# Four edits at the head of a decoder-block kernel: the bias table skewed by a replicated line in DRAM, the gate columns as one packed tile, one tile's squares on VectorE, the first key chunk between the gate products

## The reference, cut to what matters

```python
D_MODEL = 1024; SEQ = 512; N_HEADS_A = N_HEADS_B = 8; CHUNK_B = 64; CONV_B = 4
...
h = rmsnorm(x, attn_norm[i])
proj = h @ w_in[i]
qa, ka, va, qb, kb, vb, zb, bb, ab, gl = jnp.split(proj, cuts, axis=-1)
...
oa = diff_attention(qa, ka, va, lam, rel_bias)        # logits + bias_table[rel_bucket(q_pos - k_pos)]
qkv = jax.nn.silu(causal_dwconv(jnp.concatenate([qb, kb, vb], axis=-1), conv_b[i]))
qb, kb, vb = jnp.split(qkv, ...)
beta = jax.nn.sigmoid(bb)
g = -jnp.exp(a_log_b[i]) * jax.nn.softplus(ab + dt_bias_b[i])
ob = gated_delta_rule(qb, kb, vb, g, beta)            # g summed along each chunk of 64 tokens
gates = jax.nn.sigmoid(gl)
mixed = gates[:, :, 0] * (oa @ w_br_a[i]) + gates[:, :, 1] * (ob @ w_br_b[i])
x = x + mixed @ w_out[i]
x = x + (jax.nn.silu(ug) * uv) @ w_down[i]            # ug, uv from a second norm, w_up and a conv
x = x + jax.nn.sigmoid(h @ w_ple_gate[i]) * (p[i] @ w_ple_proj[i])
```

## Time and profile before

| | |
|---|---|
| median of 3 runs | 1159.39 us |
| all runs | 1157.6, 1159.39, 1159.72 us |
| the profiled execution | 1160.82 us, of which its span is 1159.0 us |
| busy | TensorE 1123.9 us, VectorE 655.2, GpSimd 633.1, ScalarE 549.4 |
| the chain that ended last | TensorE 87%, VectorE 9%, ScalarE 3% |
| line 562, the three-pass matmuls | 75% of that chain |

### The profile page before, as it was taken

One profiled execution on the slowest core, in us unless ns is written; L12 is line 12 of the kernel. 1 busy time (PEld: TensorE's weight loads), 2 busy tenths in 40 slices (PEclk: granted clock), 3 DMA queues, 4 the chain that ended last, 5 costly groups with the idle time before them and its releaser, 6 DMA issues.

```text
span 1159.0 us, 16765 instructions
## 1 busy us (share of the span) xinstructions
PE 1123.9 (97%) x5502; PEld 898.7 (78%) x5502; DVE 655.2 (57%) x1036; ACT 549.4 (47%) x886; POOL 633.1 (55%) x769
## 2 busy tenths in 40 slices
PE   6998989999999999999999999999999999999997
PEld 4786667777777777667878888888888888888886
DVE  4668976767666776862213324476776515731534
ACT  5584647566565656551322124544444314433542
POOL 6386264546554564645456554566576754573452
PEclk9999999999999999999999999999999999999999
DMA  8354031331404123213223523333333432332232
GB/s 243 77 132 130 26 94 35 85 85 35 102 18 118 38 64 100 75 54 85 79 77 105 181 72 91 91 93 114 103 90 91 116 102 73 109 96 80 74 89 79
DMA packets 196619, 104.36 MB, mean 90 GB/s; under 512 B 3926, under 2 KB 195401, under 8 KB 196553
## 3 DMA queue, kind: packets, MB, share of 16 engines
q1 hardware_dynamic: 196172, 103.39, 32.0%
q10 hardware_dynamic: 381, 0.15, 0.1%
HBM read 101.40 MB, written 2.13 MB: 89 GB/s over the span
## 4 chain that ended last, share of the span: by engine, by line
PE 87%; DVE 9%; ACT 3%; issue 1%; ACTq 0%; DVEq 0%
PE bank L562 75%; PE bank L698 2%; PE bank L712 1%; DVE prod L1810 1%; DVE xs L1812 1%; PE bank L705 1%; PE bank L657 1%; DVE pr L1722 1%; PE bank L922 1%; DVE pr L1721 0%; DVE oa_lo L1978 0%; PE bank L909 0%; PE bank L919 0%; PE bank L910 0%; PE bank L913 0%
## 5 line engine op out<-in xcount | busy, mean ns | idle before, releaser
L492 POOL TENSOR_TENSOR w_lo<-w_raw,w_hi 128x256 fp32r<-128x256 f32 x692 | 549.9, 828 | 259.9 <-ACT w_hi L1074 254.2
L562 PE MATMUL bank<-hn_hi,w_hi 128*128 128x512 f32 x1000 | 408.4, 408 | 1.0 <-DVE o_a L1985 1.0
L562 PE MATMUL bank<-hn_hi,w_lo 128*128 128x512 f32 x1000 | 391.0, 391 | 0.0
L562 PE MATMUL bank<-hn_lo,w_hi 128*128 128x512 f32 x1000 | 390.4, 390 | 0.0
L562 PEld LDWEIGHTS bank<-hn_hi,w_hi 128*128 128x128 f32 x1000 | 189.0, 189 | 43.7 <-issue 9.2
L562 PEld LDWEIGHTS bank<-hn_hi,w_lo 128*128 128x128 f32 x1000 | 187.9, 188 | 40.4
L562 PEld LDWEIGHTS bank<-hn_lo,w_hi 128*128 128x128 f32 x1000 | 188.7, 189 | 34.6 <-issue 1.7
L507 POOL CAST w_hi<-w_raw 128x1024 fp32r<-128x1024 f32 x70 | 78.2, 1117 | 222.0 <-PE bank L562 131.3
L1074 ACT ACTIVATE w_hi<-w_raw 128x1024 fp32r<-128x1024 f32 x111 | 117.9, 1062 | 77.6 <-PE bank L562 69.7
L2096 DVE SCALAR_TENSOR_TENSOR u<-vr,pt,u 128x511 f32<-128x511 f32 x88 | 88.9, 1010 | 8.3 <-DVE u L2096 0.7
L2090 DVE TENSOR_TENSOR vr<-bank,rs 128x512 f32<-128x512 f32 x44 | 30.4, 692 | 72.5 <-PE bank L562 67.1
(11 more groups left out here) (308 smaller groups left out, 1643.6 us busy)
## 6 DMA issues: line engine op xcount, KB each, us to landing
w_raw<-in_w_in SPq DMA_DIRECT2D x73, 512.0 KB, 6.7
w_raw<-in_w_up SPq DMA_DIRECT2D x44, 512.0 KB, 3.8
w_raw<-in_w_down SPq DMA_DIRECT2D x16, 512.0 KB, 3.9
crow<-cum_rows_out SPq DMA_DIRECT2D x16, 256.0 KB, 5.7
w_raw<-in_w_br_a SPq DMA_DIRECT2D x8, 512.0 KB, 4.0
w_raw<-in_w_br_b SPq DMA_DIRECT2D x8, 512.0 KB, 4.0
w_raw<-in_w_out SPq DMA_DIRECT2D x8, 512.0 KB, 3.9
w_raw<-in_w_ple_gate SPq DMA_DIRECT2D x8, 512.0 KB, 4.0
```

Of the source, the lines that this page charges most:

```text
L492: ins = pool.tensor_tensor(wlo[c.slot][:, ks, :], raw[c.slot][:, ks, :], whi[c.slot][:, ks, :].bitcast(F32), ALU.subtract)
L562: mm = pe.matmul(acc, w[c.slot][:, i, :], xx[:, x0 + i, :], start=(i == 0 and n == 0), stop=last)
```

## The change

- **Order of loads.** The constants are loaded after the second tile of `x` in place of the first, and are 48 KB shorter (no flipped identity, but a small pick matrix of 16 columns). The gate columns are loaded as 16 columns only, in rows of 64 bytes; the first key chunk comes right behind them, ahead of the lines of the bias.
- **Squares.** VectorE takes the squares of the second tile of `x`; ScalarE takes the other three, and the inverse roots of the second and third tile come together, after the third tile's squares.
- **Gate columns packed.** GpSimd puts the high part of the 16 columns in columns 0 to 15 of a buffer and the low part in 16 to 31. One matmul with 32 stationary columns serves high and low: two matmuls for each row block where there were three. A matmul with the pick matrix both turns the result and adds the two halves, in place of the transpose on line 624.
- **First key between.** The first three row blocks of the gates come first, then a step of the first key chunk (in bank 1) and a row block of the gates in turn. Of the filler then stand: 2 steps; gates turned, and here the bias line (line 611, moved; its copy on VectorE moves behind the gates' additions); 5 steps; the running sums; 2 steps; the sums turned; 1 step; then the heads as before.
- **Bias.** The bias line is written to DRAM 128 times for each head (1.5 MB in one DMA, its source 8 partitions). A read whose step from partition to partition is one number less than a line puts the bias straight into `bias`. `slope`, the flipping matmuls and the copies are gone. VectorE waits for the landing after `scale_rows`.
- **Order on SyncE.** Four key chunks go ahead of the line's write, the sixth behind it; the bias is read after the loads of all keys; each row load of the running sums moves one chunk load later.

```diff
             for t in range(NT):
                 sp.dma_start(x_tok[:, t, :], ...)
-                if t == 0:
-                    sp.dma_start(sq[:, :], consts[:, 0:C_HOT * P]).then_inc(sem("consts_in"), 16)
-            load(stream.ba.at(0), w_in0, COLS["ba"])
+                if t == 1:
+                    sp.dma_start(sq[:, :], consts[:, 0:C_HOT]).then_inc(sem("consts_in"), 16)
+            sp.dma_start(raw[0][:, :, 0:16], gate_cols).then_inc(arrived[0], 16)
+            load(stream.keys.at(0), w_in0, COLS["kb"])
...
-            for n in (1, 2):
+            for n in (1, 2, 3, 4):
                 load(stream.keys.at(n), w_in0, COLS["kb"] + n * P)
             sp.wait_ge(sem("line_ready"), 1)
-            sp.dma_start(dram_line, line[:, :]).then_inc(sem("line_out"), 16)
-            sp.wait_ge(sem("line_out"), 16)
-            skew = bass.AP(tensor=dram_line.tensor, offset=0, ap=[[1, P], [LINE, H], [1, 256]])
-            sp.dma_start(slope[:, :, :], skew).then_inc(sem("slope_in"), 16)
-            for n in (3, 4):
-                load(stream.keys.at(n), w_in0, COLS["kb"] + n * P)
+            sp.dma_start(dram_line, line[:, :].unsqueeze(1).to_broadcast([H, P, LINE])).then_inc(sem("line_out"), 16)
+            load(stream.keys.at(5), w_in0, COLS["kb"] + 5 * P)
...
+            sp.wait_ge(sem("line_out"), 16)
+            skew = bass.AP(tensor=dram_line.tensor, offset=P - 1, ap=[[LINE - 1, P], [P * LINE, H], [1, 256]])
+            sp.dma_start(bias[:, :, :], skew).then_inc(sem("bias_in"), 16)
...
+            def gate_products(i):
+                pe.wait_ge(low_ready, 1)
+                pe.wait_ge(sem("h_split"), i + 1)
+                for n, xx in enumerate((hn_hi, hn_lo)):
+                    mm = pe.matmul(bank[0][0:32, :], whi[0][:, i, 0:32], xx[:, i, :], ...)
-            run(gemm(stream.ba.at(0), hn_hi, hn_lo, ready=("h_split", 0)))
+            f = Fill(gemm(stream.keys.at(0), hn_hi, hn_lo, ready=("h_split", 0)))
+            for i in range(3):
+                gate_products(i)
+            for i in range(KD):
+                f.step(1)
+                if i + 3 < KD:
+                    gate_products(i + 3)
...
             for t in range(NT):
-                mm = pe.transpose(bank[5][:, t * 16:t * 16 + 16], ba_sb[:, t * P:(t + 1) * P], ident[0:16, 0:16])
+                mm = pe.matmul(bank[5][:, t * 16:t * 16 + 16], ba_sb[:, t * P:(t + 1) * P], pick[0:32, :], ...)
             mm.then_inc(sem("ba_T"), 1)
-            f.step(6)
+            pe.matmul(bank[6][0:H, 0:LINE], tab[:, :], hot[:, :], start=True, stop=True).then_inc(sem("line_mm"), 1)
+            f.step(5)
             pe.wait_ge(sem("ba_gates"), 4)
...
-            f.step(2)
-            pe.wait_ge(sem("slope_in"), 16)
-            for n in range(H // 2):
-                pe.matmul(bank[6 + n % 2][:, :], flip, slope[:, 2 * n:2 * n + 2, :]..., ...)
-            f.step(4)
+            f.step(1)
...
-            for t in range(NT):
+            for n, (t, t0) in enumerate(((0, 0), (2, 1), (3, 3))):
                 act.wait_ge(sem(f"x_in{t}"), 16)
                 link(nc.scalar.activation(junk[:, :], x_tok[:, t, :], ACT.Square, accum_out=ss0[:, t:t + 1]))
...
+            dve.wait_ge(sem("x_in1"), 16)
+            done(V.scalar_tensor_tensor(out=junk1[:, :], in0=x_tok[:, 1, :], scalar=1.0, in1=x_tok[:, 1, :],
+                                        op0=ALU.mult, op1=ALU.mult, accum_out=ss0[:, 1:2]), "x_sq", 1)
...
-                if h == 0:
-                    for n in range(H // 2):
-                        bias_copy(n)
```

More of the change, by code:

```diff
@@ L190, in const @@
             return sq[:, n * P:(n + 1) * P]
-        ident, flip, cum, half, ones, mask = map(const, range(6))
+        ident, cum, half, ones, mask = map(const, range(5))
+        pick = sq[:, C_PICK:C_HOT]
         LOW, UP = slice(0, HEAD), slice(HEAD, P)
@@ L229, in build @@
         lamp = sb("lamp", [P, 2, 64], F32, first)
-        ba_sb = sb("ba_sb", [16, T], F32, first)
+        ba_sb = sb("ba_sb", [32, T], F32, first)
         cum_rows = sb("cum_rows", [NT * H, P], F32, first)
-        junk = sb("junk", [P, D], F32, first)
+        junk, junk1 = (sb(n, [P, D], F32, first) for n in ("junk", "junk1"))
         alog = sb("alog", [P, H], F32, first)
@@ L608, in _ @@
                         mm.then_inc(sem("x_T"), 1)
-            pe.wait_ge(sem("lines_in"), 16 * 2)
-            pe.wait_ge(sem("eps_set"), 4)
-            pe.matmul(bank[6][0:H, 0:LINE], tab[:, :], hot[:, :], start=True, stop=True).then_inc(sem("line_mm"), 1)
             for c in range(len(IN_BANKS), KD):
@@ L616, in _ @@
                 mm.then_inc(sem("x_T"), 1)
-            run(gemm(stream.ba.at(0), hn_hi, hn_lo, ready=("h_split", 0)))
-            f = Fill(*[gemm(stream.keys.at(n), hn_hi, hn_lo) for n in range(H)],
+            def gate_products(i):
+                pe.wait_ge(low_ready, 1)
+                pe.wait_ge(sem("h_split"), i + 1)
+                for n, xx in enumerate((hn_hi, hn_lo)):
+                    mm = pe.matmul(bank[0][0:32, :], whi[0][:, i, 0:32], xx[:, i, :],
+                                   start=(i == 0 and n == 0), stop=(i == KD - 1 and n == 1))
+                if i == KD - 1:
+                    mm.then_inc(product_ready, 1)
+            f = Fill(gemm(stream.keys.at(0), hn_hi, hn_lo, ready=("h_split", 0)))
[5 more added lines that the diff above has]
+                    gate_products(i + 3)
+            f = Fill(*[gemm(stream.keys.at(n), hn_hi, hn_lo) for n in range(1, H)],
                      *[gemm(stream.first.at(n), hn_hi, hn_lo) for n in range(len(FIRST))])
@@ L623, in _ @@
             for t in range(NT):
-                mm = pe.transpose(bank[5][:, t * 16:t * 16 + 16], ba_sb[:, t * P:(t + 1) * P], ident[0:16, 0:16])
+                mm = pe.matmul(bank[5][:, t * 16:t * 16 + 16], ba_sb[:, t * P:(t + 1) * P], pick[0:32, :], start=True, stop=True)
             mm.then_inc(sem("ba_T"), 1)
-            f.step(6)
+            pe.wait_ge(sem("lines_in"), 16 * 2)
+            pe.wait_ge(sem("eps_set"), 4)
+            pe.matmul(bank[6][0:H, 0:LINE], tab[:, :], hot[:, :], start=True, stop=True).then_inc(sem("line_mm"), 1)
+            f.step(5)
             pe.wait_ge(sem("ba_gates"), 4)
@@ L1094, in _ @@
             act.wait_ge(sem("eps_set"), 3)
[L1095 removed]
+            for n, (t, t0) in enumerate(((0, 0), (2, 1), (3, 3))):
                 act.wait_ge(sem(f"x_in{t}"), 16)
                 link(nc.scalar.activation(junk[:, :], x_tok[:, t, :], ACT.Square, accum_out=ss0[:, t:t + 1]))
[L1098 to L1099 removed]
+                if t == 2:
+                    act.wait_ge(sem("x_sq"), 1)
+                these = slice(t0, t + 1)
+                link(nc.scalar.activation(lnx[:, these], ss0[:, these], ACT.Ln, bias=sm[:, 28:29], scale=1.0 / D))
+                done(nc.scalar.activation(rs0[:, these], lnx[:, these], ACT.Exp, scale=-0.5), "x_r", n + 1)
             act.wait_ge(sem("pt_ready"), 1)
@@ L1626, in _ @@
             for c in range(KD):
-                if c == 2:
-                    dve.wait_ge(sem("line_mm"), 1)
-                    done(V.tensor_copy(line[:, :], bank[6][0:H, 0:LINE]), "line_ready", 1)
                 dve.wait_ge(sem("h_high"), c + 1)
@@ L1658, in _ @@
                                  dtb[:, :].unsqueeze(1).to_broadcast([P, NT, H]), ALU.add), "ba_gates", 3)
+            dve.wait_ge(sem("line_mm"), 1)
+            done(V.tensor_copy(line[:, :], bank[6][0:H, 0:LINE]), "line_ready", 1)
             dve.wait_ge(sem("soft"), 4)
```

59 lines of the change are left out of this document (28 added, 31 removed).

## The result

| | before | after |
|---|---|---|
| median, on one chip | 1159.2 us | 1190.94 us (4 runs, 1189.39 to 1193.03) |
| span of the profiled execution | 1159.0 us | 1187.6 us |
| mean granted clock | 0.995 | 0.984 |

The ratio is 1.0279, 95% interval 1.0264 to 1.0293: 31.7 us slower, far above the forecast and above its range.

The account below looks back on a forecast made before the run. TensorE, busy 97%, was taken to bound the kernel except where the first key's chain ends last. First key products -0.05, S +0.2, clock and third products +1.3 made +1.5: 1160.9 us against the median 1159.39; range 1158.0 to 1164.0.

Parts of the forecast that it names:

- The line's write: On SyncE's queue ahead of the sums' write: the 1.5 MB bias line write takes 8 us, between 5.5 and 14, no cost.
- The rule beside it: On SyncE's queue: the line's write delays the sums only if over 9 us, then costs 1 us per us.
- The upper end: For the line's write: 14 us, six times the 2.3 us of the 256 KB `out` store; it would cost 5 us.
- the rival: On SyncE's queue: the line's write blocks the sums, costing up to 5 us, 1162 to 1166 us; chance 0.21.
- The sign that the prediction named for itself: Ahead of the first decay matrix: if ScalarE waits for `crow` there, the forecast is wrong; no size given.
- The key-0 chain ends last: At the first key products: the first key is ready at S + 24.2, leaving TensorE 3.9 us idle.
- S: The start of the gate products, 19.16 us before the change; the prediction measures the first key products from it.
- The saving of TensorE's work: From S to the first key products: 3.5 us less TensorE work, with 3.9 us of idle time taking its place.
- The pick products: In turning the gates: 8 instructions replace four transposes, adding between nothing and 0.9 us; 0.1 taken.
- The clock fell: Behind the idle time ahead of the key products: the granted clock falls, costing 0 to 1.7 us; 1.4 taken.
- The start: Up to the gate products: the new load order and squares move S by -0.2 to +0.6 us; +0.2 taken.
- that case: The forecast's sum with no cost from the line's write: +1.5 us, from -0.05, +0.2 and +1.3.

## Why the prediction was wrong, step by step

- **The line's write: the step that failed.** I bounded it by 5.5 and 14 us from the store of `out` and took 8; it took about 33. The rule beside it was right: "it decides from a write over 9 us and costs 1 us per us" gives 24 us for 33, and the third key products came 24.7 us late. The upper end was no bound, because the row it came from reads all of its source partitions, and this write reads 8 of them 128 times each. I had put "8 source partitions, 128 copies" down as what speaks for the rival without giving it a price. At 6.1 GB/s for each source the rival was the case, with 0.21 of the chance and an end of 5 us that was five times too low. The sign that the prediction named for itself came: ScalarE waits for `crow` ahead of the first decay matrix, 24.4 us.
- **The Trainium skill** (DMA: Bandwidth & Descriptors, "Rules for kernel authors") speaks against the change, and the share of 0.46 agrees with its 8 engines of 16. The 9.2 us that the prediction estimates with it, for a write at half rate, don't agree with about 33: 16 engines at a share of 0.92 still moved only 97 GB/s, so with few sources the number of engines isn't what holds the write.
- **The key-0 chain ends last.** First key products at S + 24.2 forecast, 43.21 - 18.79 = S + 24.42 measured; a wait of 3.9 us forecast, 3.62 measured, on the line named. The saving of TensorE's work bought nothing, as forecast. On the way: the turned sums' copy at 37.60, S + 18.8 (S + 18.55). That it fits so well is in part luck. The pick products were mis-sized, 1.06 us for eight against 0.42 for the four transposes before, where I took 0.1 more; they lie on the chain, and VectorE had the gates at 31.23, S + 12.4 instead of 11.9. From there to the end of the gates' last step, line 1663 before and 1680 now, were 3.79 us (to 35.02) instead of 4.27, which took it back.
- **The clock fell** behind that wait: 51.26 - 43.21 = 8.05 us between the first two key products, 6.35 before, so 1.7 (I took 1.4). The second stretch at the 1.2 GHz level, behind the wait of 23 us, cost more: from the third key products to the fourth 8.26 us. Here the Trainium skill (TensorE: Matmul & The Clock Gate, "Why this matters for your kernels"), which warns of idle gaps between bursts, and the trace agree. Waits shorter than that rule names did it too: behind the 2.13 us with key 0's convolution first the granted clock was 0.50 at 58 to 60, behind the 2.21 us with the old bias path 0.50 at 41 to 43.
- **The start** was wrong in sign and small: S at 18.79, -0.37 instead of +0.2; the third tile of `x` landed at 8.5 where I had 9.4, the fourth's squares began at 10.59 and not at 11.1. The third tile's squares wait on their load, as forecast (0.51 us). It isn't steady: 18.42 to 19.64 over the variants of the changed kernel, with the first gate products at 0.63 us each instead of 0.39 in those where TensorE's clock was still at the low level.
- **A term that wasn't there: the tiles' place**, 2.2 us in the trace. I had read "48 KB shorter" in the change as a shorter load and not as a move of every tile behind it. (It is 56 KB, 384 to 328, 448 bytes in each partition.) "The rest of the program is the same" is true of its instructions and not of where its tiles lie.

The sum closes: 24.7 us at the third key products; 26.6 at the eighth (114.70 against 88.11), by the low clock; 26.2 at the first matmul of the attention (135.12 against 108.92); 2.2 from 515 us on; 28.6 at the end. The last 3.1 us are the choice of execution: the one of before lay 1.6 us over the median of 1159.2, and the one of after, its quickest, 1.5 under its own.

Without the write and the place of the tiles the changed kernel is still 1.0042 of before, 4.9 us, and 1.5 were forecast for that case. In the profile of the padded kernel with 128 sources (an execution 2.8 us over its median) the key products begin 1.9 us late (S at 19.47 and the low clock behind it), and the stretch at the low level behind them costs 2.75 us (45.36 to 54.46) instead of 1.7. It is 4.2 us behind at the first matmul of the attention and 5.1 at the end. The clock was 0.992 or 0.993 in all five runs, 0.994 to 0.996 before. So the rest goes, as far as this trace shows, to TensorE's waits and what they do to the clock; no run takes all of them away, so this part is argued and not shown. Whether it is the first wait or the later ones isn't settled either: taking the first away only moved it. Nothing tried here beat the kernel before.

## What to carry to other kernels

Price a DMA that repeats its source by how many partitions it reads and how often it reads each, not by the bytes of the nearest store; then look at who stands behind it in the queue, and know that another queue gave back only 7 us of 25 here. When an edit changes the size of one tile, keep the tiles behind it at their offset modulo 256 bytes, or pad, and measure (one kernel and three shifts are behind this): a slower stream of matmuls shows in no wait, only in the distance between the first and the last of them. A microsecond saved on TensorE is worth something only behind the point where the other engines' chain catches up, and of such chains there may be a second one right behind the first. Before moving a step later, look at what its reading sets free: with two buffers, the next copy can go out only then.

## What the runs showed of the hardware

- Reading one partition again and again, a DMA from SBUF to DRAM moved 6.1 to 6.3 GB/s for each source partition (50, 97 and 196 GB/s from 8, 16 and 32, each read 128, 64 and 32 times), while 128 sources, read 8 times each, gave 325 GB/s and more.
- While such a write of 8 sources ran on ScalarE's queue, a store of 16 KB on SyncE's took 15.7 us, alone 1.4.
- Matmuls of 128x512 on operands 64 bytes off a multiple of 256 (counted from their place in the kernel before) took 2.4 ns longer each in a stream without waits, 128 bytes off 6.7 ns, 256 bytes off nothing. Of such a matmul's own operands only the 512 columns had moved, its weights hadn't; which of the moved tiles does it, the one read or another engine's, wasn't tried.
- The skewed read of the bias, 1 MB, took 11.4 us from issue to landing in the changed kernel and 8.6 to 13.1 in its variants; with the old bias path a skewed read of the same size took 5.7.
